# Two experts with fixed rows, a new pass plan, and a last pass interleaved with the reload of the expert outputs

## The reference

```python
def grouped_moe(h, w_router, router_bias, w1, w3, w2):
    T, D = h.shape
    scores = jax.nn.sigmoid((h @ w_router).astype(jnp.float32))
    ...
    _, expert = lax.top_k(masked, TOP_K)          # TOP_K = 2 of N_EXPERTS = 16
    gw = jnp.take_along_axis(scores, expert, axis=1)
    gw = gw / jnp.sum(gw, axis=-1, keepdims=True)
    ...
    def expert_block(args):
        xb, e = args
        return (jax.nn.silu(xb @ w1[e]) * (xb @ w3[e])) @ w2[e]
    ...
    return jnp.zeros((T, D), h.dtype).at[tok_sorted].add(ys[dest] * g_sorted[:, None].astype(h.dtype))

# in reference(), for each of the 2 layers
        h = rms_norm(x, norm2[l]) * (1.0 + sc2) + sh2
        x = x + g2 * grouped_moe(h.reshape(B * S, D), w_router, router_bias,
                                 w1[l], w3[l], w2[l]).reshape(B, S, D)
    return rms_norm(x, norm_f)
```

## Time and profile before

| what | value |
|---|---|
| median of 3 runs | 1576.4 us (1575.21 to 1576.48) |
| the profiled execution, its own time | 1578.35 us |
| its span | 1576.5 us |
| PE busy | 1476.3 us (94%) |
| DVE busy | 575.3 us (36%) |
| ACT busy | 427.8 us (27%) |
| mean granted clock of TensorE | 0.972 of full speed |
| moved by DMA | 346.83 MB, mean 220 GB/s |

### The profile page before, as it was taken

The page is one execution under the profiler, slowest core; times in us unless marked ns, Lnnn a source line. Parts: engine busy times, 40 slices in busy tenths (PEclk is TensorE's granted clock), DMA queues, the critical chain, the costliest instruction groups (busy, mean ns, idle before and its releaser), DMA issues.

```text
span 1576.5 us, 19611 instructions
## 1 busy us (share of the span) xinstructions
PE 1476.3 (94%) x7572; PEld 801.5 (51%) x7573; DVE 575.3 (36%) x1343; ACT 427.8 (27%) x980; POOL 86.9 (6%) x96
## 2 busy tenths in 40 slices
PE   5998999999999699999989899999999949999996
PEld 1664555677754333444346555666776423334442
DVE  0056554575643401111154464463333250111115
ACT  2326564300012112111141565551000121111111
POOL 0000002000000001000000000020000000111000
PEclk8999999999999699999999999999999969999998
DMA  9625163225260799999962432501304239999994
GB/s 361 231 82 201 43 228 120 81 66 148 67 253 27 298 418 422 420 422 423 381 238 107 140 132 89 179 1 41 106 1 165 83 139 419 420 419 423 421 409 174
DMA packets 94872, 346.83 MB, mean 220 GB/s; under 512 B 13722, under 2 KB 37882, under 8 KB 80376
## 3 DMA queue, kind: packets, MB, share of 16 engines
q1 hardware_dynamic: 69152, 305.68, 49.5%
q0 software_dynamic: 8976, 31.46, 5.4%
q10 hardware_dynamic: 16648, 8.40, 1.8%
HBM read 331.55 MB, written 21.00 MB: 224 GB/s over the span
## 4 chain that ended last, share of the span: by engine, by line
PE 87%; DMA 5%; DVE 4%; ACT 2%; issue 1%; DVEq 1%; SPq 0%; POOLq 0%; ACTq 0%
PE bank L2035 18%; PE bank L1773 12%; PE bank L1723 10%; PE bank L2046 9%; PE bank L1941 7%; PE bank L1815 7%; PE bank L1830 5%; PE bank L1840 4%; PE bank L1850 4%; DMA ring<-in_w 2%; PE bank L1756 2%; PE bank L1654 2%; PE bank L1687 2%; PE bank L2001 1%; DMA ring<-in_w_ada 1%
## 5 line engine op out<-in xcount | busy, mean ns | idle before, releaser
L2035 PE MATMUL bank<-ring,reg_b 128*32 128x512 f32 (+2 forms) x1376 | 284.3, 609 | 3.0 <-ACT reg_b L1082 3.0
L2035 PEld LDWEIGHTS bank<-ring,reg_b 128*32 128x32 f32 (+2 forms) x1376 | 94.2, 129 | 141.5 <-issue 137.2
L1723 PE MATMUL bank<-ring,hT 128*128 128x512 f32 (+3 forms) x512 | 159.2, 472 | 2.4 <-ACT hT L915 2.4
L1723 PEld LDWEIGHTS bank<-ring,hT 128*128 128x128 f32 x512 | 97.8, 192 | 59.3 <-issue 32.5
L2046 PE MATMUL bank<-ring,reg_b 128*32 128x512 f32 (+2 forms) x576 | 127.3, 594 | 0.0
L1815 PE MATMUL bank<-reg_a,ring 128*128 128x512 f32 x256 | 112.6, 593 | 0.9 <-issue 0.9
L1941 PE MATMUL bank<-ring,reg_b 128*128 128x512 f32 x256 | 113.0, 596 | 0.0
L1082 ACT ACTIVATE reg_b<-bank,cur 128x128 f32<-128x128 f32 x176 | 64.0, 469 | 177.6 <-PE bank L2001 177.6
L994 ACT ACTIVATE reg_f<-bank,nmax 128x512 f32<-128x512 f32 x128 | 87.2, 685 | 61.4 <-DVE nmax L1292 60.3
L1292 DVE TENSOR_REDUCE nmax<-bank 128x1 f32<-128x512 f32 x128 | 83.7, 685 | 51.2 <-PE bank L1830 51.2
L1773 PE MATMUL bank<-hT,ring 128*128 128x256 f32 x384 | 88.1, 379 | 0.0
(11 more groups left out here) (292 smaller groups left out, 1812.1 us busy)
## 6 DMA issues: line engine op xcount, KB each, us to landing
ring<-in_w SPq DMA_DIRECT2D x76, 2048.0 KB, 23.3
ring<-in_w_ada SPq DMA_DIRECT2D x19, 2048.0 KB, 7.4
ring<-in_w_in SPq DMA_DIRECT2D x10, 2048.0 KB, 19.1
hT<-in_w SPq DMA_DIRECT2D x10, 2048.0 KB, 27.9
reg_a<-in_w SPq DMA_DIRECT2D x10, 2048.0 KB, 21.6
vb<-in_w_ada ACTq DMA_DIRECT2D x16, 512.0 KB, 4.0
ring<-in_w_o SPq DMA_DIRECT2D x4, 2048.0 KB, 8.6
ring<-in_w_proj_a SPq DMA_DIRECT2D x8, 512.0 KB, 10.7
```

Of the source, the lines that this page charges most:

```text
L1723: ins = pe.matmul(bank[z_bank(k)][:, 0:n], hT[:, c, t * P:(t + 1) * P], w[:, c, :], start=c == 0, stop=c == NC - 1)
L2035: ins = pe.matmul(bank[bk][at:at + n, :], xsT[:, p % 2, c, at:at + n], slot(MOE_SLOT[j, m], NC, F)[:, c, :], start=c == 0, stop=c == NC - 1)
```

## The change

1. **Places and passes.** Experts 11 and 12 have fixed rows (places 0 and 1); the other 14 are ranked, and ranking now works on arrays of 16 and not of 15, with the two fixed experts forced to the last ranks. `TILES`, `EXPERT_RANK` and `MOE_LOADS` are new. There are 11 passes as before.
2. **Loads.** The six loads of the fixed experts are issued before the order is known. When it is, w1 and w3 of the first ranked place are issued at once. The wait of SP for the first gather (`xg_s[0]`) is gone.
3. **Last pass.** In pass 10 the PE does the w2 products of pass 9 between w1 and w3 of pass 10. The blocks 0 and 1 of the expert outputs are read back when pass 9 has been scattered, blocks 2 and 3 after `h3_r` of pass 10, before the flag of `extra_blocks` is read. DVE adds block 0 to x ahead of `put_out` of pass 10 and a half of block 1 behind it. Where extra blocks run, the blocks are read again and added with weights `gw_over`, which hold the pairs beyond the rows.
4. **Final norm.** DVE adds all outputs to x first (semaphore `fx_s`); the PE then copies x to PSUM and adds the last pass there, ACT squares from PSUM and DVE scales from PSUM.

```diff
-EXPERT_RANK = (None, 13, 5, 6, 7, 8, 9, 10, 0, 1, 11, 12, 2, 3, 4, 14)
-TILES = (((0, 0, 32), (0, 32, 32), (0, 64, 32), (1, 96, 32)),
-         ((2, 0, 32), (2, 32, 32), (2, 64, 32), (3, 96, 32)),
+STATIC = (11, 12)
+EXPERT_RANK = (14, 15, 9, 0, 4, 5, 10, 1, 8, 13, 2, 6, 7, 11, 12, 3)
+TILES = (((0, 0, 32), (0, 32, 32), (0, 64, 32), (1, 96, 32)),
+         ((1, 0, 64), (2, 64, 64)),
...
-                load_w1(0, 0)
-                load_w3(0, 0)
-                wait(sp, ya_r, l * 8 + 8)
-                load_w2(0, 0)
+                load_w2(0, STATIC[0])
+                load_w1(1, STATIC[1])
+                wait(sp, ya_r, l * 8 + 8)
+                load_w2(1, STATIC[1])
+                wait(sp, yb_r, l * 8 + 8)
+                load_w1(0, STATIC[0])
+                wait(sp, wo_r, l * 8 + 8)
+                load_w3(0, STATIC[0])
+                wait(sp, lp4_r, l * NT + NT)
+                load_w3(1, STATIC[1])
                 wait(sp, ord_s, l + 1)
...
-                wait(sp, yb_r, l * 8 + 8)
-                rank[1] = expert_at(1)
-                load_w1(1, rank[1])
-                wait(sp, xg_s[0], l * (16 * gathers(0)) + 16)
-                wait(sp, wo_r, l * 8 + 8)
-                load_w3(1, rank[1])
                 rank[2] = expert_at(2)
+                wait(sp, xn_st, l * 64 + 64)
                 load_w1(2, rank[2])
+                load_w3(2, rank[2])
                 rank[3] = expert_at(3)
-                wait(sp, lg_r, l * NT + NT)
+                wait(sp, h1_r, l * PASSES + 1)
                 load_w1(3, rank[3])
...
+                def load_outputs(t, done):
+                    sp.dma_start(cy[t].rearrange("p k n -> p (k n)"), ys_d.rearrange("(t p k) n -> t p (k n)", p=P, k=2)[t]).then_inc(done, 16)
+                for b in range(2):
+                    wait(sp, ys_st[b], (l + 1) * (16 * scatters(b)))
+                wait(sp, y_r, (l * PASSES + PASSES - 1) * 2)
+                for t in range(2):
+                    load_outputs(t, cg_s[t])
+                wait(sp, h3_r, l * PASSES + PASSES)
+                for t in range(2, NT):
+                    load_outputs(t, cg_s[t])
...
-                    if e < PASSES:
-                        hidden(l * PASSES + e)
-                    if e >= 1:
+                    if e == PASSES - 1:
+                        hidden(l * PASSES + e, between=out_before)
+                    elif e < PASSES:
+                        hidden(l * PASSES + e)
+                        if e >= 1:
+                            out_before()
+                    else:
+                        add_outputs(l, 0)
+                        out_before()
+                        if l < DEPTH - 1:
+                            add_output(l, 1, 0)
...
                     for m, done in ((0, h1_r), (1, h3_r)):
+                        if p == PASSES - 1 and m == 1:
+                            pe.wait_ge(tr_e, g)
+                            pe.wait_ge(y_e, (l * PASSES + p - 1) * 2)
+                            down_tiles(p - 1)
```

More of the change, by code:

```diff
@@ L169, in constants @@
     first, rows = rows_by_rank()
[L170 to L173, removed]
-                c[:, C_ST + j] = P * p + min(a for i, a, _ in tiles if i == j)
-    c[:, C_BC:C_BC + RANKED] = first
-    c[:, C_BC + RANKED:C_BC + 2 * RANKED] = rows
+    c[:, C_BC:C_BC + E] = first
+    c[:, C_BC + E:C_BC + 2 * E] = rows
     return c
@@ L248, in trunk @@
         gw = sb("gw", [P, 2, NT])
+        gw_over = sb("gw_over", [P, 2, NT])
         table = sb("table", [P, 2 * E], i32)
@@ L482, in trunk @@
         cg_s = [sem(f"token_outputs_loaded{t}") for t in range(NT)]
+        cx_s = [sem(f"token_outputs_with_extra_blocks_loaded{l}") for l in range(DEPTH)]
+        fx_s = sem("final_x_in_sbuf")
         ov_free = sem("extra_block_done")
@@ L525, in extra_blocks @@
                             eng.reg_add(blocks, blocks, 1)
+                if finish is not None:
+                    finish()
         @block.sync
@@ L763, in body, with all_outputs @@
                     sp.dma_start(slot(5, 4, D), w2_v[l * E + e]).then_inc(ov_w, 16)
+                def all_outputs():
+                    wait(sp, ov_all, l + 1)
+                    for t in range(NT):
+                        load_outputs(t, cx_s[l])
                 wait(sp, fl_s, l + 1)
[L765 to L772 removed]
+                extra_blocks(sp, n_ov, n_tab, body, finish=all_outputs)
                 wait(sp, y_r, (l * PASSES + PASSES) * 2)
@@ L867, in body @@
                     wait(pool, ov_free, n + 1)
+                    for t in range(2, NT):
+                        wait(pool, cg_s[t], l * 16 + 16)
                     pool.tensor_copy(idx[:, 0:1], table[:, bass.ds(e, 1)]).then_inc(ov_i, 1)
@@ L1116, in _ @@
             for t in range(NT):
-                act.wait_ge(x2, DEPTH * NT + t + 1)
-                square(2 * DEPTH, t)
+                for h, (total, done) in enumerate(((lsum, sqh_s), (ssq, sq_s))):
+                    act.wait_ge(lp_r, ((DEPTH - 1) * NT + t) * 2 + h + 1)
+                    A(sq_j[:, h * 512:(h + 1) * 512], bank[last_bank(DEPTH - 1, t) + h][:, :], ACT.Square,
+                      accum_out=total[:, t:t + 1]).then_inc(done, 1)
                 root(2 * DEPTH, t)
@@ L1553, in _, with hidden @@
                 v.tensor_copy(flag_i[:, :], r_s[0:1, 160:161]).then_inc(fl_s, 1)
-                def hidden(at):
+                def hidden(at, between=None):
                     v.wait_ge(sge_s, at + 1)
                     TT(u_s, bank[4][:, :], sg_e, ALU.mult)
+                    if between is not None:
+                        between()
                     v.drain()
@@ L1627, in _ @@
                     v.drain()
-                    STT(xn[:, u, :], x[:, u, :], rstd[:, u:u + 1], nf_row, ALU.mult, ALU.mult).then_inc(out_s, 1)
+                    for h in range(2):
+                        cols = slice(h * 512, (h + 1) * 512)
+                        ins = STT(xn[:, u, cols], bank[last_bank(DEPTH - 1, u) + h][:, :], rstd[:, u:u + 1], nf_row[:, cols], ALU.mult, ALU.mult)
+                    ins.then_inc(out_s, 1)
         @block.tensor
@@ L1660, in last_pass @@
                     pe.wait_ge(wt_s, layer + 1)
-                elif layer < DEPTH - 1 and t >= 2:
+                if layer == DEPTH - 1:
+                    pe.wait_ge(fx_s, t + 1)
+                elif t >= 2:
                     pe.wait_ge(x2, (layer + 1) * NT + (1 if t == 2 else 3))
@@ L1664, in last_pass @@
                     cols = slice(h * 512, (h + 1) * 512)
-                    own = layer == DEPTH - 1 and t > 0
+                    own = layer == DEPTH - 1
                     dst = bank[last_bank(layer, t) + h][:, :]
```

234 lines of the change are left out of this document (115 added, 119 removed), and 13 rows, old and new, of the table MOE_LOADS.

## The result

The changed kernel takes 1632.4 us (median of 4 runs, 1631.1 to 1633.2), the kernel before 1576.4 beside it: a ratio of 1.0356 (1.0338 to 1.0374), 56 us slower. The prediction was 1583.0 with a range from 1572 to 1590; the sign was right and the size was not. The profiled execution has a span of 1630.3 us in place of 1576.5.

The account below looks back on a forecast made before the run. It took the PE as the bound, busy 94%, with DMA also near its limit and gains left only before and behind the passes. First layer +6.1 and second +0.5 gave +6.6 us on 1576.4: 1583.0 us, range 1572 to 1590.

Parts of the forecast that it names:

- What changes nothing: Expert passes: still 11, side-by-side tiles take the time of one, no extra block runs; the new cut is worth nothing.
- First gather: Start of each layer: the gather queues behind a whole extra load and lands later, +4.5 us a layer; floor +0.3.
- my second rival: The gather passes between the loads, costing +0.3 us in each layer: 1574.6 us; chance 0.12.
- Removed waits: Pass 1: the waits for w3 of place 3 go away, -1.0 us in the first layer, -0.6 in the second.
- Late weights: Near the end of the passes: w2 of place 12 is issued late and tight, 0.5 us for each layer.
- End of the first layer: Block 0 lands at 792.9 with `put_out` queued behind its additions; first layer +6.1 us, gather and removed wait included.
- Rearranged pass: Pass 10: w2 products of pass 9 only change places, and the exposed multiply ends before block 0 lands; costs nothing.
- Final part: End of the second layer: block 0 added early, `put_out` 0.9 us later, end at 1569.5 against 1573.4: -3.9 us.
- Ranking: Ahead of the table, on the path to the first gather: ranking over 16 costs up to 0.4 us, taken as 0.3.
- The first rival: Block 0's reload lands before 783 in the first layer: 1576 with late gather (0.08), 1567 with free one (0.08).
- The third: Rival: weights come late at the end of the passes, two loads ahead, 4.5 us in each layer: 1590; chance 0.13.

Follow-up runs that it names:

- the run with one width: The changed kernel with pass 9 cut as four tiles of 32 rows (place 12 as two of 32): 1590.8 us, ratio 1.0089 to the kernel before.
- the three points above: Gather with two, one or no loads beside it: the run with one width 1590.8 us, SP's wait between its ranked loads 1581.9, ahead of both 1577.8.
- both ways of taking the wait away: On the kernel with the gather wait: first layer's `put_out` ahead of block 0's additions, 1579.1 us; or third part of w_in behind the reload, 1578.3 us.
- the kernel with the gather wait: The run with one width plus SP's wait for the first gather between the two ranked loads: 1581.9 us, ratio 1.0023 to the kernel before.

## Why the prediction was right or wrong

**The step that failed** is under "What changes nothing": *a pass of tiles side by side takes the time of one, so the new cut of the passes is worth nothing.* It holds for tiles of one width, which is all that the trace of before could show: there a place of 96 rows is cut as three tiles of 32 wherever it stands beside one of 32. Pass 9 of the new plan is the first with 64 beside 32, and costs 26.7 us a layer. The trace could not give that price, but the change's own `TILES` shows the new form, and no row stood behind the claim that it is free. A form that before does not have should have been bounded: tiles one after the other are twice the time of a pass, 21 us a layer. None of the rivals held this case.

**The terms beside it**, read from the run with one width. Its span is 11.9 us over the span before, in place of +6.6: by the table +9.6 in the first layer (forecast +5.8), -0.4 between, +4.7 in the second (forecast +0.2), and -1.9 because this trace's first gather was issued earlier, which no edit explains.

- *First gather, +4.5 a layer:* 10.4 and 11.3 us against 5.7 and 5.5 before, +4.7 and +5.8. Mechanism right, shown by the three points above, and size right in the first layer, 1.3 short in the second. The rule by which a gather would pass between two loads ("DMA: Bandwidth & Descriptors" of the Trainium skill, section "Queues, rings and completion order"), my second rival, did not hold for the gathers beside two loads.
- *Removed waits, -1.0 and -0.6:* right; none is left in pass 1.
- *Late weights, +0.5 a layer:* w2 of places 11 and 12, which I had watched, came late by 0.9 and 0.4, and w2 of place 14, which I had only as a rival, by 1.8 and 2.1. Before had one such wait, of 1.9 in the first layer, so the second layer pays 2.5. Undersized by 2.0.
- *End of the first layer:* the place was right (block 0 behind the last products, `put_out` behind it), and both ways of taking the wait away gave 3 to 4 us. Undersized by 3.8, the late weights of that layer included: the block landed 1.9 us later after the gather's issue than forecast, and from landing to the normed block 12.5 us pass in place of 10.6, as the clock had fallen.
- *Rearranged pass, 0:* no cost beside that of the exposed multiply (next term) was seen, and undone in the kernel with the gather wait it cost 17 us.
- *Final part, -3.9:* about -2.5. From `put_out` to the end the changed kernel is 3.5 us shorter, where the forecast had 23.4 - 18.5 = 4.9, and both are to be lessened by what `put_out` comes later (forecast 0.9, measured about 1.0: the w2 products of pass 10 start 2.1 us behind the products ahead of them, before 1.1). DVE waits 1.4 and 1.0 us for ACT's squares, which I had called faster than DVE.
- *Ranking, +0.3:* the PE's two waits for the table grew by 0.6 us in sum.

The first rival, the reload in time, is what the changed kernel shows by accident, since the slow pass 9 made the time for it. The third, late weights, came in a small form. The point at which the first gather is issued differs by up to 3.7 us between the traces (522.6 to 526.3) without an edit ahead of it, so one profile is no measure below that; the ratios are.

## What to carry to other kernels

Ask of each plan whether it holds a *form* that the profile of before does not, and give that form a price from both sides. Tiles of the PE array that stand side by side should have one width: cut the wide one down, which cost nothing here (64 rows as two tiles of 32). And a load issued "as early as possible" is paid by whatever short transfer is on the path beside it; hold it until the short one has landed, if its weights are not wanted in the very next pass.

## What the runs showed of the hardware

That tiles of 64 and of 32 columns, next to each other in the PE's order, don't run side by side (1.98 us a chunk in place of 0.87), and that this is no gap in the trace but busy time, so that the share of 94% is the same in both kernels. And that a second load beside a gather costs it 4 to 5 us where the first costs 1 to 2.
